# Second feed-forward network: the first four chunks turned, split and multiplied one token tile at a time

## What is computed

```
x = x + rms_norm(memory_cross_attention(...), post_x_g)
h = rms_norm(x, pre_ffn_g)
f = square(relu(h @ w_ff1)) @ w_ff2        # w_ff1 1024 x 4096, w_ff2 4096 x 1024
x = x + rms_norm(f, post_ffn_g)
```

## Time and profile before

| | us |
|---|---|
| median of 3 runs | 788.99 (788.84 to 789.08) |
| the profiled execution | 789.57 |
| its span, first to last instruction | 787.7 |
| PE busy in the span | 773.3 (98%) |
| DVE busy | 569.0 (72%) |
| ACT busy | 436.8 (55%) |

### The profile page before, as it was taken

The page is one execution under the profiler, slowest core; times in us unless marked ns, Lnnn a source line. Parts: engine busy times, 40 slices in busy tenths (PEclk is TensorE's granted clock), DMA queues, the critical chain, the costliest instruction groups (busy, mean ns, idle before and its releaser), DMA issues.

```text
span 787.7 us, 11513 instructions
## 1 busy us (share of the span) xinstructions
PE 773.3 (98%) x4504; PEld 672.0 (85%) x4504; DVE 569.0 (72%) x776; ACT 436.8 (55%) x652; POOL 76.1 (10%) x128
## 2 busy tenths in 40 slices
PE   6999999999999999999999999999999999999997
PEld 4999877888898888888899997889988988888885
DVE  4996999859787567676667999657647666665664
ACT  5555487675665444444465477656646644444452
POOL 5023930000010000000010000100001100000001
PEclk9999999999999999999999999999999999999999
DMA  9988998945457686866556554446423766666651
GB/s 322 367 266 302 358 314 298 339 162 162 132 162 240 193 298 196 272 215 178 168 189 213 167 163 155 159 137 214 160 87 105 221 201 190 187 190 194 190 174 54
DMA packets 84533, 163.35 MB, mean 207 GB/s; under 512 B 5424, under 2 KB 15856, under 8 KB 84480
## 3 DMA queue, kind: packets, MB, share of 16 engines
q1 hardware_dynamic: 82656, 157.31, 61.6%
q10 hardware_dynamic: 1424, 4.81, 1.8%
q0 software_dynamic: 400, 0.50, 0.4%
HBM read 161.55 MB, written 1.05 MB: 206 GB/s over the span
## 4 chain that ended last, share of the span: by engine, by line
PE 93%; DVE 2%; ACT 2%; issue 1%; DMA 1%; SPq 0%; POOL 0%; DVEq 0%; ACTq 0%; POOLq 0%
PE bank L1852 20%; PE bank L1853 20%; PE bank L1854 20%; PE bank L1921 13%; PE bank L1924 7%; PE bank L1865 2%; PE bank L1871 2%; PE bank L1867 2%; DVE ada_acc L1044 1%; PE bank L1974 1%; PE bank L2549 1%; PE bank L2125 1%; DMA ada_ring<-in_w_ada 1%; PE bank L2148 1%; PE bank L2012 0%
## 5 line engine op out<-in xcount | busy, mean ns | idle before, releaser
L1014 DVE TENSOR_TENSOR lo_ring<-raw_ring,hi_ring 128x1024 fp32r<-128x1024 f32 x247 | 302.9, 1231 | 151.2 <-ACT hi_ring L540 150.5
L540 ACT CAST hi_ring<-raw_ring 128x1024 fp32r<-128x1024 f32 x248 | 259.5, 1051 | 246.8 <-PE bank L1854 145.9
L1852 PE MATMUL bank<-hi_ring,branch_hi 128*128 128x512 f32 x352 | 139.0, 395 | 0.0
L1853 PE MATMUL bank<-lo_ring,branch_hi 128*128 128x512 f32 x352 | 137.2, 390 | 0.0
L1854 PE MATMUL bank<-hi_ring,branch_lo 128*128 128x512 f32 x352 | 137.0, 389 | 0.0
L1921 PE MATMUL bank<-h_hi_lo,hi_ring 128*128 128x512 f32 x448 | 111.8, 391 | 0.0
L1921 PEld LDWEIGHTS bank<-h_hi_lo,hi_ring 128*128 128x128 f32 x448 | 81.3, 189 | 15.1
L1854 PEld LDWEIGHTS bank<-hi_ring,branch_lo 128*128 128x128 f32 x352 | 66.1, 188 | 14.0
L1852 PEld LDWEIGHTS bank<-hi_ring,branch_hi 128*128 128x128 f32 x352 | 66.2, 188 | 13.9 <-issue 0.8
L1853 PEld LDWEIGHTS bank<-lo_ring,branch_hi 128*128 128x128 f32 x352 | 66.2, 188 | 13.4 <-issue 0.5
L1852 PE MATMUL bank<-h_hi_lo,hi_ring 128*128 128x256 f32 x240 | 69.1, 288 | 0.0
(11 more groups left out here) (299 smaller groups left out, 1166.7 us busy)
## 6 DMA issues: line engine op xcount, KB each, us to landing
raw_ring<-in_w_ff SPq DMA_DIRECT2D x128, 512.0 KB, 3.7
raw_ring<-in_w_in SPq DMA_DIRECT2D x64, 512.0 KB, 4.9
raw_ring<-in_w_out SPq DMA_DIRECT2D x16, 512.0 KB, 3.3
raw_ring<-in_w_xkv SPq DMA_DIRECT2D x16, 512.0 KB, 3.6
mem_v<-in_w_ada SPq DMA_DIRECT2D x13, 512.0 KB, 5.3
mem_k<-in_w_ada SPq DMA_DIRECT2D x11, 512.0 KB, 5.8
ada_ring<-in_w_ada SPq DMA_DIRECT2D x8, 512.0 KB, 7.0
raw_ring<-in_w_branch SPq DMA_DIRECT2D x8, 512.0 KB, 3.7
```

What stands on the lines that cost most here:

```text
L540: act.copy(m.hi[:, m.slot(u)], m.raw[:, m.slot(u)]).then_inc(s.hi_done, 1)
L1014: dve.tensor_tensor(m.lo[:, m.slot(u)], m.raw[:, m.slot(u)], as_f32(m.hi[:, m.slot(u)]), ALU.subtract).then_inc(s.lo_done, 1)
L1852: pe.matmul(out, a_hi, b_hi, start=start, stop=False, skip_group_check=True)
L1853: pe.matmul(out, a_hi, b_lo, start=False, stop=False, skip_group_check=True)
```

## The change

It concerns chunks 0 to 3 (`LEAD = 4`) at the start of the second network; the rest of the program stays.

- PE: `keep_busy` and its six products are gone. `lead_tiles` turns chunks 0 to 3 of token tile 0 into bank 2, then chunks 4 to 7 of it into banks 6 and 7. It then multiplies chunks 0 to 2 of tile 0 (eight products of 128 columns each) before the first turns of tile 1, chunk 3 of tile 0 between the two groups of turns of tile 1, and chunks 0 and 1 of tile 1 after them. The products with the low part of `h` stay 256 wide and come after a pair's high ones. The third and fourth unit go through `leading` as before.
- ACT: the high parts of chunks 0 to 3 are written in two pieces of 128 tokens, the pieces of tile 0 ahead of the cast of a weight unit.
- DVE: their low parts in pieces too, tile 0 and tile 1 of a pair of chunks in turn.

```diff
+LEAD = 4
 (ACT)
+    act.wait_ge(s.lead_turned, 1)
+    for k in range(LEAD):
+        act.activation(m.h_hi[:, k, 0:P], m.lead_ps(k), ACT.Copy, scale=lead_gain(k)).then_inc(s.lead_hi, 1)
     after(FF2 - 2)
-    gain_hi(s.ff2t, cols[:, G_FF2:G_FF2 + KD], m.h_hi, single=0)
+    for k in range(LEAD):
+        if k % 2 == 0:
+            act.wait_ge(*s.ff2t.turned.at(k // 2 + 1))
+        act.activation(m.h_hi[:, k, P:S], m.chunk_ps(k)[:, P:S], ACT.Copy,
+                       scale=lead_gain(k)).then_inc(s.ff2t.hi.sem, 1)
+    gain_hi(s.ff2t, cols[:, G_FF2:G_FF2 + KD], m.h_hi, range(2, 4))
 (DVE)
-    gain_lo(s.ff2t, cols[:, G_FF2:G_FF2 + KD], m.h_hi, m.h_lo, range(0, 2), single=0)
+    dve.wait_ge(s.lead_hi, LEAD)
+    for b in range(LEAD // 2):
+        for k in (2 * b, 2 * b + 1):
+            lead_part(k, m.lead_ps(k), slice(0, P)).then_inc(s.lead_lo, 1)
+        dve.wait_ge(*s.ff2t.hi.at(2 * b + 2))
+        for k in (2 * b, 2 * b + 1):
+            lead_part(k, m.chunk_ps(k)[:, P:S], slice(P, S)).then_inc(s.ff2t.lo.sem, 1)
 (PE)
-            if tt:
-                keep_busy(idle)
...
+    def lead_tiles(u0, t, post):
+        def passes(k, tok):
+            pe.wait_ge(s.lo_done, u0 + k // UK + 1)
+            slot = m.slot(u0 + k // UK)
+            for f in range(4):
+                fc = slice(f * P, f * P + P)
+                out = bank[f // 2][:, (f % 2) * S + tok.start:(f % 2) * S + tok.stop]
+                pe.matmul(out, m.hi[:, slot, k % UK, fc], m.h_hi[:, k, tok], start=k + tok.start == 0 and f % 2 == 0,
+                          stop=False, skip_group_check=True)
+                pe.matmul(out, m.lo[:, slot, k % UK, fc], m.h_hi[:, k, tok], start=False, stop=False, skip_group_check=True)
...
+        claim(2, 4, 5, 6, 7)
+        pe.wait_ge(*post.x.at(1))
+        for k in range(LEAD):
+            ins = pe.transpose(m.lead_ps(k), m.x[:, 0, k * P:k * P + P], m.ident[:, :])
+        ins.then_inc(s.lead_turned, 1)
+        free[2] = s.lead_lo, LEAD
+        pe.wait_ge(*post.x.at(2))
+        transposes(t, m.x, 0, range(LEAD, KD))
+        claim(0, 1)
+        for k in range(LEAD - 1):
+            first_passes(k)
+        pe.wait_ge(*post.x.at(3))
+        transposes(t, m.x, 1, range(LEAD))
+        first_passes(LEAD - 1)
+        pe.wait_ge(*post.x.at(4))
+        transposes(t, m.x, 1, range(LEAD, KD))
...
+        for u in range(LEAD // UK):
+            for k in (UK * u, UK * u + 1):
+                pe.wait_ge(*t.hi.at(k + 1))
+                passes(k, slice(P, S))
+            for k in (UK * u, UK * u + 1):
+                pe.wait_ge(s.lead_lo, k + 1)
+                pe.wait_ge(*t.lo.at(k + 1))
+                for f in range(4):
+                    mm = pe.matmul(bank[f // 2][:, (f % 2) * S:(f % 2) * S + S],
+                                   m.hi[:, m.slot(u0 + u), k % UK, f * P:f * P + P], m.h_lo[:, k, :], start=False,
+                                   stop=False, skip_group_check=True)
+            mm.then_inc(s.used, 1)
```

More of the change, by code:

```diff
@@ L321, in __init__ @@
         self.xq_hi, self.xq_out = [new("xq_hi0"), new("xq_hi1")], [new("xq_out0"), new("xq_out1")]
+        self.lead_turned, self.lead_hi, self.lead_lo = new("lead_turned"), new("lead_hi"), new("lead_lo")
         self.r_logit, self.r2_ok = new("r_logit"), new("ff2_scale")
@@ L435, in tall, with lead_ps @@
         return ring[:, u % RING].rearrange("p k n -> p (k n)").rearrange("p (k n) -> p k n", n=S)
+    def lead_ps(self, k):
+        return self.bank[2][:, k * P:k * P + P]
     def chunk_ps(self, k):
@@ L994, in act_program, with lead_gain @@
         post_square(s.post_x, n, 1, 2 * n + 1)
-    after(FF2 - 2)
-    gain_hi(s.ff2t, cols[:, G_FF2:G_FF2 + KD], m.h_hi, single=0)
+    def lead_gain(k):
+        return cols[:, G_FF2 + k:G_FF2 + k + 1]
+    act.wait_ge(s.lead_turned, 1)
+    for k in range(LEAD):
+        act.activation(m.h_hi[:, k, 0:P], m.lead_ps(k), ACT.Copy, scale=lead_gain(k)).then_inc(s.lead_hi, 1)
+    after(FF2 - 2)
+    for k in range(LEAD):
[4 more added lines that the diff above has]
+    gain_hi(s.ff2t, cols[:, G_FF2:G_FF2 + KD], m.h_hi, range(2, 4))
     after(FF2 - 1)
@@ L1656, in dve_program, with lead_part @@
             after(XO + XO_AHEAD + 1)
-    gain_lo(s.ff2t, cols[:, G_FF2:G_FF2 + KD], m.h_hi, m.h_lo, range(0, 2), single=0)
+    def lead_part(k, ps, tok):
+        return dve.scalar_tensor_tensor(out=m.h_lo[:, k, tok], in0=ps, scalar=cols[:, G_FF2 + k:G_FF2 + k + 1],
+                                        in1=as_f32(m.h_hi[:, k, tok]), op0=ALU.mult, op1=ALU.subtract)
+    dve.wait_ge(s.lead_hi, LEAD)
[5 more added lines that the diff above has]
+            lead_part(k, m.chunk_ps(k)[:, P:S], slice(P, S)).then_inc(s.ff2t.lo.sem, 1)
     after(FF2 - 2)
@@ L1976, in transposes @@
                 ins.then_inc(turn.turned.sem, 1)
[L1978 to L1983, removed]
     def turn_normed(turn, ahead=None):
@@ L1993, in turn_normed, with turn_x @@
                 transposes(turn, m.norm, tt, range(i * n, i * n + n))
-    def turn_x(turn, post, idle=0):
+    def turn_x(turn, post):
         claim(4, 5, 6, 7)
         for tt in range(NT):
-            if tt:
-                keep_busy(idle)
             for n in range(2):
@@ L2308, in gate_row, with first_passes @@
             free[0], free[1] = (s.ff_row, 1), (s.ff_row, 3)
+    def lead_tiles(u0, t, post):
[8 more added lines that the diff above has]
+                pe.matmul(out, m.lo[:, slot, k % UK, fc], m.h_hi[:, k, tok], start=False, stop=False, skip_group_check=True)
+        def first_passes(k):
+            pe.wait_ge(s.lead_hi, k + 1)
+            passes(k, slice(0, P))
+        claim(2, 4, 5, 6, 7)
[14 more added lines that the diff above has]
+        transposes(t, m.x, 1, range(LEAD, KD))
+        for b in range(4):
+            free[4 + b] = t.lo.at(2 * b + 2)
+        for u in range(LEAD // UK):
[10 more added lines that the diff above has]
+            mm.then_inc(s.used, 1)
     def feed_forward(f, t, post, beside=None):
@@ L2321, in feed_forward @@
         u = f.u0
-        claim(0, 1)
-        for q in range(RING):
+        if f is s.ff2:
+            lead_tiles(u, t, s.post_x)
+        else:
+            claim(0, 1)
+        for q in range(LEAD // UK if f is s.ff2 else 0, RING):
             leading(u + q, q, m.h_hi, m.h_lo, FF_LEAD[0], t)
@@ L2598, in pe_program @@
         free[2 * n + tt] = s.post_x.scaled.at(s.post_x.nth(n, tt))
-    turn_x(s.ff2t, s.post_x, idle=6)
-    for b in range(4):
-        free[4 + b] = s.ff2t.lo.at(2 * b + 2)
     feed_forward(s.ff2, s.ff2t, s.post_ff2)
```

## The result

| | before | after |
|---|---|---|
| median, us | 789.05 | 790.68 |
| ratio | 1 | 1.0022 (95% interval 1.0016 to 1.0028) |
| span of the profiled execution | 787.7 | 789.5 |
| first turn of tile 0 to first product of the next slab | 15.60 | 17.31 |

Both medians are of 18 runs in turn on one chip. The kernel became 1.6 us slower by the medians, 1.3 to 2.2 by the interval, which is just above what can be told from no change. The forecast was 790.5, 1.5 us more.

A forecast was written before the change was run, and what follows sets the result against it. PE, busy 98% of the span, was taken as the bound. Narrow products +3.26, hole −1.40 and turns −0.38 gave +1.48 us, thus 790.5 us against the median of 788.99; range 789.3 to 791.4.

The forecast's parts named there:

- Where the bound lies: Whole kernel: PE is busy 98% of the span, so a microsecond lost or won at the change arrives whole.
- 1. Idle products out, price 0: PE before tile 1's turns: removing six idle products costs 0, as PE has nothing else to do then.
- 2. The early start: PE on tile 0: ACT's first piece takes 0.40, so PE starts at 602.52 and its first product streams at 602.63.
- 3. The narrow product: Lead chunks on PE: 64 narrow products at 0.111 replace 32 wide ones at 0.120, +3.26 us.
- 4. The hole: PE's wait before tile 1's turns: narrow products stream from 602.63 instead of idling until 604.03, −1.40 us.
- 5. The turns: Tile 1's turns on PE: two groups between products take 0.80 instead of 1.18, −0.38 us.
- 6. The sum: Whole lead on PE: +1.48 us, the next slab starting at 618.2 instead of 616.7.
- 7. The others: ACT, DVE, SP and POOL around the lead: their moved work stays hidden behind PE, no term.
- A: Lead block on PE: each narrow product pays a full wide slot of 0.12, +2.06 us, 791.05; chance 0.18.
- B: Lead block on PE: loads hide behind the previous stream, products cost 0.060 to 0.080, 787.2 to 788.5 us; chance 0.12.
- C: Narrow block on PE: clock falls or a new wait appears, +7 us at half clock, 797 or more; joint chance 0.06.
- D: PE's early products don't start before 604.03 because ACT is late, +2.9 us; counted in the joint chance 0.06.

The follow-up runs named there:

- the run on the order of waits: The changed kernel with PE waiting for the weight unit's low part first, once for two chunks: 790.61 us, ratio 1.0018.
- The table of 8, 12 and 16: The changed kernel with two lead chunks and only 8, 12 or 16 early narrow products: 789.14, 789.13 and 789.47 us.

## Why the prediction held, point by point

**Where the bound lies.** A difference of 1.71 us in the stretch became 1.8 us of span. Held.

**1. Idle products out, price 0.** Wrong as a statement on the kernel before. They fill a wait there, but without them 6 of 21 runs are longer by 1.4 us or more, with a lower clock as the likely cause. It cost this forecast little, since the changed kernel's early narrow products shorten the hole to 602.1 to 602.8. Whether it is wholly free of falls stays open: 2 of its 18 runs are at 792.15 and 792.28, 1.5 us above the others, at a mean clock of 0.997 against 0.998 or more, and no profile caught one.

**2. The early start.** Forecast 1.41 us after the first turn (602.52 − 601.11), measured 1.60. ACT's piece was even shorter than the 0.40 taken. What was mis-sized is the way from ACT to PE, 0.04 in the sum: the first piece is done at about 602.55 (602.18 + 0.37), and PE's first load starts at 602.77.

```profile
602.77 0.19 PEld L2334 LDWEIGHTS bank<-h_hi_lo,hi_ring 128*128 128x128 f32 x1 [0.77 <-DVE gates L1147]
```

(DVE's L1147, which the row names, is no cause: of its two products the first was over at 602.18, and the second ends at 602.87, after the load's start.) In between, the trace has two waiting instructions of PE, 0.05 long each: L2339 at 602.59, the wait for the piece, and L2329 at 602.69, the wait for the weight unit. The first follows ACT by the 0.04 of the sum. From it to the second 0.11 passes, and from there to the load 0.08; neither had a term. With one such instruction in place of two, in the run on the order of waits, PE starts 0.11 earlier, and the 0.08 remains. The start was 0.19 late, but only 0.09 of it reaches the sum, which had set 0.11 for the first load in front of the stream: the first product starts 0.03 behind its load. Counted back from the turns at 605.50, 24 slots of 0.112 begin 1.61 after the first turn (605.50 − 601.20 − 2.69), where the sum had 1.52 (602.63 − 601.11).

**3. The narrow product.** Taken 0.111, measured 0.112; the term is 3.33 instead of 3.26. The decision against the column bound of 0.060 was right, and the two experiments on columns show it; that the load makes the 0.11 is the reading that fits best. The Trainium skill's 81 ns a product in a stream of 128 columns ("TensorE: Matmul & The Clock Gate", section "Back-to-back issue gap") isn't borne out here, where they stand 112 ns apart; the 107 ns of its section "LDWEIGHTS (loading the stationary operand)" is close to what 64 and 128 columns measure. What the sum lacked is small: from the first wide product behind narrow ones to the second the distance is 0.17 instead of 0.12, which happens twice, and from the first narrow one behind wide ones to the second it is 0.06 (610.00 to 610.06) instead of 0.11, once.

**4. The hole.** Taken −1.40. With the start of step 2 it is −(2.92 − 1.61) = −1.31, where 2.92 is the start of the turns of tile 1 after the first turn in the kernel before (604.03 − 601.11).

**5. The turns.** From 605.39 to 606.03 lie four turns and two narrow steps: 0.64 − 0.22 = 0.42 a group, at 0.40 taken. The term is −0.34 instead of −0.38.

**6. The sum.** 3.33 − 1.31 − 0.34 = 1.68, measured 1.71, forecast 1.48. So 0.23 was missing: 0.09 in the start, 0.07 in the product's price (0.001 too low, 64 times), 0.04 in the turns, 0.03 at the passages between wide and narrow. All four err to the same side, which is why the result fell just outside the 0.2% within which the forecast stood.

**7. The others.** No engine made PE wait. The table of 8, 12 and 16 shows one more miss: 16 early products measured 0.17 over their sum. Most of it is the turns: eight in one row take 0.91 in that trace (604.69 to 605.60), and the sum had the 0.80 of two groups between products; 0.05 is at the passage from narrow to wide.

**The rivals.** A (a full wide slot for each) is refuted: 256 columns instead of 128 cost 0.56 more. B (a narrow product costs 0.060 to 0.080) is refuted by the 0.112, and by 64 columns costing the same as 128. C was given 0.06 together with D and a price of +7. In the changed kernel it decides nothing, but as a mechanism it is real: +1.5 behind an empty hole, +6 to +8 with 64 columns. Against it I had set a hole of 0.72 us at 15.19; one such hole at full clock didn't show that a hole of 2 us is harmless. D didn't occur.

## What to carry to other kernels

Cutting a product along its moving columns doubles the number of products and weight loads, and with weights of 128x128 in this rounded float32 type each costs 0.11 us, nearly the whole 0.12 of 256 columns: an early half leaves a late half that costs nearly as much as the whole did. So a wait of PE is worth filling in this way only with the few products that fit into it, and gains a tenth of a microsecond here at best. Before taking out work that seems idle, look at the times and the granted clock of several runs, not of one profile: its use may show in a third of them only.

## What I had not expected

- The granted clock fell to 0.50 (1.2 GHz) behind a PE hole of 2.1 us, as the profile of one kernel shows, and was back at 1.00 from about 608.2. By their times it did so in 7 of 10 runs of that kernel and in 3 of 10 and 3 of 11 of one with the same hole. With six idle products in the hole the profile has 1.00 throughout, and ten of eleven runs lie within 0.35 us.
- With 64 columns a product instead of 128, weights, waits and distances unchanged, it fell in 7 of 10 runs, and in the profiled one it stood at 0.50 from about 605 to 622. With 256 columns, in the same batch, none of 8 runs is high. PE's row was full around the fall (2.00 of 2.00 us in 604 to 606), so a full row doesn't show that the clock will hold.
- The distance of two products is 0.11 at 64 columns, 0.112 at 128 and 0.120 at 256.
